# A bisection for the 256th largest index score: the wide tiles' search starts seven steps earlier, VectorE counts one of them, and the exact last step goes in pieces

## What is computed

```python
def dsa_attention(q, k, v, iq, ik, iw, table):
    ...
        logits = jnp.einsum('bqhd,bkd->bqhk', iqb, ik).astype(jnp.float32) * (IDX_DIM ** -0.5)
        score = jnp.einsum('bqhk,bqh->bqk', jax.nn.relu(logits), iwb)
        score = jnp.where(kpos[None, None, :] <= qpos[None, :, None], score, NEG)
        _, idx = lax.top_k(score, topk)
        valid = idx <= qpos[None, :, None]
    ...
        p = jax.nn.softmax(s, axis=-1)
```

## Time and profile before

| | us |
|---|---|
| median of 3 executions | 3599.42 (3598.71 to 3608.11) |
| the profiled execution's own time | 3598.85 |
| its span, first to last instruction | 3597.1 |
| TensorE busy | 3436.0 (96%) |
| VectorE busy | 1601.4 (45%) |
| ScalarE busy | 978.1 (27%) |
| mean granted TensorE clock | 0.983 of full |
| the loop of 64 steps, from the span's start | 1762.4 to 2398.6 |

### The profile page before, as it was taken

How to read it: one execution, slowest core, us unless ns; L and a number is a source line. 1 busy time by engine, 2 the same in 40 slices (tenths; PEclk the granted TensorE clock), 3 DMA queues, 4 the chain that set the end, 5 groups by cost and what they waited for, 6 DMA issues and landing times.

```text
span 3597.1 us, 31176 instructions
## 1 busy us (share of the span) xinstructions
PE 3436.0 (96%) x12370; PEld 1812.8 (50%) x12370; DVE 1601.4 (45%) x2938; ACT 978.1 (27%) x2059; POOL 93.6 (3%) x107
## 2 busy tenths in 40 slices
PE   7999999999999999999999999899999999999998
PEld 3556555555456444544566455564444444444443
DVE  2056191143156362552465563654336555253433
ACT  4244112002244111122577744531111000000001
POOL 0000000020000000100000000000110000000000
PEclk9999999999999999999999999899999999999999
DMA  5100121131000101111000101111000111101011
GB/s 209 54 6 13 58 88 62 53 108 38 27 7 13 34 27 53 41 44 41 36 24 30 39 21 56 62 45 44 29 24 35 47 47 35 47 35 47 35 41 65
DMA packets 49903, 163.72 MB, mean 46 GB/s; under 512 B 5296, under 2 KB 8624, under 8 KB 49085
## 3 DMA queue, kind: packets, MB, share of 16 engines
q1 hardware_dynamic: 44890, 145.82, 11.5%
q10 hardware_dynamic: 4868, 15.91, 1.3%
HBM read 157.46 MB, written 11.32 MB: 47 GB/s over the span
## 4 chain that ended last, share of the span: by engine, by line
PE 86%; DVE 7%; ACT 4%; issue 1%; SPq 1%; DMA 0%; POOL 0%; DVEq 0%; ACTq 0%; POOLq 0%
PE ps L551 34%; PE ps L1220 14%; PE ps L580 8%; PE ps L992 5%; PE ps L708 4%; PE ps L1003 2%; PE ps L731 2%; PE ps L887 2%; PE ps L720 2%; PE ps L1015 1%; PE ps L1070 1%; ACT sb L1756 1%; PE ps L1081 1%; DVE sb L2000 1%; PE ps L977 1%; PE ps L1098 1%
## 5 line engine op out<-in xcount | busy, mean ns | idle before, releaser
L551 PE MATMUL ps<-sb 128*128 128x512 f32 (+1 forms) x3088 | 1240.9, 563 | 14.0 <-ACT sb L1559 6.7
L551 PEld LDWEIGHTS ps<-sb 128*128 128x128 f32 x3088 | 589.3, 191 | 659.3 <-issue 633.8
L1279 ACT ACTIVATE sb<-ps 128x512 f32<-128x512 f32 (+10 forms) x709 | 350.6, 511 | 1522.9 <-PE ps L551 467.3
L1220 PE MATMUL ps<-sb 128*128 128x512 f32 x1232 | 531.3, 594 | 2.8 <-DVE sb L2626 2.8
L1220 PEld LDWEIGHTS ps<-sb 128*128 128x128 f32 x1232 | 234.6, 191 | 299.0 <-issue 293.5
L580 PE MATMUL ps<-sb 128*128 128x512 f32 x672 | 291.4, 594 | 2.4 <-ACT sb L1279 1.9
L992 PE MATMUL ps<-sb 128*128 128x512 f32 x512 | 231.3, 599 | 0.0
L580 PEld LDWEIGHTS ps<-sb 128*128 128x128 f32 x672 | 127.3, 190 | 163.2 <-issue 156.1
L1321 ACT ACTIVATE sb<-sb 128x512 f32<-128x512 f32 x128 | 74.7, 610 | 366.0 <-DVE sb L2573 122.5
L2136 DVE SCALAR_TENSOR_TENSOR sb<-sb 128x1310 f32<-128x1310 f32 (+1 forms) x120 | 161.7, 1424 | 0.0
L708 PE MATMUL ps<-sb 96*128 96x512 f32 (+1 forms) x400 | 155.3, 523 | 5.2 <-ACT sb L1468 4.5
(11 more groups left out here) (258 smaller groups left out, 3148.9 us busy)
## 6 DMA issues: line engine op xcount, KB each, us to landing
sb<-in_w_in SPq DMA_DIRECT2D x73, 512.0 KB, 3.3
sb<-in_w_ada SPq DMA_DIRECT2D x48, 512.0 KB, 4.6
sb<-in_w_up SPq DMA_DIRECT2D x44, 512.0 KB, 3.3
sb<-in_w_down SPq DMA_DIRECT2D x24, 384.0 KB, 3.1
sb<-in_w_out SPq DMA_DIRECT2D x16, 512.0 KB, 3.6
sb<-in_w_mkv SPq DMA_DIRECT2D x16, 512.0 KB, 3.3
rows_dram<-vec_dram ACTq DMA_DIRECT2D x1, 6906.0 KB
sb<-rows_dram ACTq DMA_DIRECT2D x6, 1024.0 KB, 5.1
```

The lines of the kernel that those rows point to most:

```text
L551: ins = mm(ps[:, 0:tn], w[:, k, :], src(k, t0, tn), start=(k == 0), stop=(k == nk - 1))
L1220: ins = mm(ps[:, 0:512], stationary(k), moving(k), start=(first and k == 0), stop=(k == 3), skip_group_check=not first)
L1279: return act(out, in_, func, scale=scale)
```

## The change

The group "high" begins at step 16, so that its passes fill steps 16 to 48. VectorE counts tile 7 (1024 columns) as it already counts tile 5, by the same instruction on the same scratch tile `marks`; ScalarE keeps tiles 2, 3, 4 and 6. `narrow` treats the last tile of either group in an instruction of its own. `keep_ranked` becomes a generator that stops after "at least", after the settling, and after each part but the last. `rank_pieces` advances it by two pieces ahead of `combine` or `normalise` and by one piece behind them, from step 34, 36, 38, 40, 50 and 53 on for tiles 2 to 7. Every write of the scratch tile waits for the last writer before it (`marked`). What is computed stays the same.

```diff
-SEARCH_AT = {"low": 0, "high": 23}
+SEARCH_AT = {"low": 0, "high": 16}
 PASSES = 33
-COUNTED = 5
-RANKED_AT = {34: 2, 36: 3, 38: 4, 40: 5, 57: 6, 59: 7}
+COUNTED = {"low": 5, "high": 7}
+RANKED_AT = {34: 2, 36: 3, 38: 4, 40: 5, 50: 6, 53: 7}
...
             count_signs("low", n, (4,))
-            count_signs("high", n, (6, 7))
+            count_signs("high", n, (6,))
...
-            if COUNTED in tiles:
-                j = COUNTED - 2
-                v.tensor_tensor(met[:, 0:j], tally[:, 0:j], goal[:, 0:j], ALU.is_ge).then_inc(*e.step())
-                stt(out=met[:, j:j + 1], in0=tally[:, j:j + 1], scalar=sense[:, j:j + 1], in1=goal[:, j:j + 1], op0=ALU.mult,
-                    op1=ALU.is_ge).then_inc(*e.step(("met", group, i)))
-            else:
-                v.tensor_tensor(met[:, g], tally[:, g], goal[:, g], ALU.is_ge).then_inc(*e.step(("met", group, i)))
+            a, j = g.start, COUNTED[group] - 2
+            v.tensor_tensor(met[:, a:j], tally[:, a:j], goal[:, a:j], ALU.is_ge).then_inc(*e.step())
+            stt(out=met[:, j:j + 1], in0=tally[:, j:j + 1], scalar=sense[:, j:j + 1], in1=goal[:, j:j + 1], op0=ALU.mult,
+                op1=ALU.is_ge).then_inc(*e.step(("met", group, i)))
...
-        def count_least(n):
+        marked = [None]
+
+        def mark(key):
+
+            marked[0] = key
+            return e.step(key)
+
+        def count_least(group, n):
...
+            e.wait_ge(*at(marked[0]))
+            v.tensor_scalar(marks[:, 0:w], sel(t), limit[group] if i else 0.0, 0.0, ALU.is_ge, ALU.add,
+                            accum_out=tally[:, j:j + 1]).then_inc(*mark(("counted", group, i, t)))
...
-        def keep_ranked(n):
-
-            if n not in RANKED_AT:
-                return
-            t = RANKED_AT[n]
+        ranking = [None]
+
+        def rank_pieces(n, pieces):
+
+            for _ in range(pieces):
+                if ranking[0] is None and n in RANKED_AT and ("sel", RANKED_AT[n]) not in steps.at:
+                    ranking[0] = keep_ranked(RANKED_AT[n])
+                if ranking[0] is not None and next(ranking[0], "kept") == "kept":
+                    ranking[0] = None
+
+        def keep_ranked(t):
+
...
+                if name == "at least":
+                    yield
...
             for p, (a, w) in enumerate(parts):
+                yield
...
             for piece in FILLERS.get((n, 0), ()):
                 filled(*piece)
+            rank_pieces(n, 2)
             if n < 32:
                 combine(n)
...
-            keep_ranked(n)
-            count_least(n)
+            rank_pieces(n, 1)
+            count_least("low", n)
+            count_least("high", n)
             if 1 <= n <= 32:
                 divide(n - 1)
```

More of the change, by code:

```diff
@@ L389, in program @@
     bound, found, power, tally, goal, met, sense, above, below, gap = [small[:, 128 + 6 * i:134 + 6 * i] for i in range(10)]
-    at_least, beyond, is_above, rank_value, rank_left, limit = [small[:, 188 + i:189 + i] for i in range(6)]
+    at_least, beyond, is_above, rank_value, rank_left = [small[:, 188 + i:189 + i] for i in range(5)]
+    limit = {"low": small[:, 193:194], "high": small[:, 194:195]}
     marks = view(KB0 + 2560, 256).bitcast(I8)
@@ L2259, in narrow @@
                     j, w = t - 2, (t + 1) * P
-                    v.tensor_scalar(met[:, j:j + 1], tally[:, j:j + 1], float(TOPK if t == COUNTED else 2 * TOPK - w), None,
+                    v.tensor_scalar(met[:, j:j + 1], tally[:, j:j + 1], float(TOPK if t == COUNTED[group] else 2 * TOPK - w), None,
                                     ALU.is_ge).then_inc(*e.step(("met", group, 0, t)))
@@ L2265, in narrow @@
                     v.tensor_scalar(sense[:, j:j + 1], met[:, j:j + 1], 2.0, -1.0, ALU.mult, ALU.add).then_inc(*e.step())
-                    span, low = (2 * TOPK - 1, 1 - TOPK) if t == COUNTED else (4 * TOPK - 2 * w - 2, w - 2 * TOPK + 2)
+                    span, low = (2 * TOPK - 1, 1 - TOPK) if t == COUNTED[group] else (4 * TOPK - 2 * w - 2, w - 2 * TOPK + 2)
                     v.tensor_scalar(goal[:, j:j + 1], met[:, j:j + 1], float(span), float(low), ALU.mult, ALU.add).then_inc(
@@ L2312, in narrow @@
             v.tensor_scalar(below[:, g], below[:, g], -1.0, None, ALU.mult).then_inc(*e.step(("turned ends", group)))
-        def count_least(n):
-            i, t = n - SEARCH_AT["low"], COUNTED
+        marked = [None]
[3 more added lines that the diff above has]
+        def count_least(group, n):
+            i, t = n - SEARCH_AT[group], COUNTED[group]
             if not 0 <= i < PASSES:
@@ L2322, in count_least @@
             else:
[L2323 to L2328, removed]
+                e.wait_ge(*at(("bound", group, i)))
+                stt(out=limit[group], in0=bound[:, j:j + 1], scalar=-1.0, in1=sense[:, j:j + 1], op0=ALU.mult,
+                    op1=ALU.mult).then_inc(*e.step(("limit", group, i)))
+                e.wait_ge(*at(("limit", group, i)))
+            e.wait_ge(*at(marked[0]))
+            v.tensor_scalar(marks[:, 0:w], sel(t), limit[group] if i else 0.0, 0.0, ALU.is_ge, ALU.add,
+                            accum_out=tally[:, j:j + 1]).then_inc(*mark(("counted", group, i, t)))
         def parts_of(t):
             return [(a, min(256, (t + 1) * P - a)) for a in range(0, (t + 1) * P, 256)]
-        def keep_ranked(n):
-            if n not in RANKED_AT:
-                return
-            t = RANKED_AT[n]
+        ranking = [None]
[6 more added lines that the diff above has]
+        def keep_ranked(t):
             j, x, parts = t - 2, sel(t), parts_of(t)
@@ L2347, in keep_ranked @@
                         e.wait_ge(*at(("at least", t, len(parts) - 1)))
+                    e.wait_ge(*at(marked[0]))
                     v.tensor_scalar(equal[:, 0:w], x[:, a:a + w], above[:, j:j + 1], total if p else 0.0, compare, ALU.add,
-                                    accum_out=total).then_inc(*e.step((name, t, p)))
+                                    accum_out=total).then_inc(*mark((name, t, p)))
+                if name == "at least":
+                    yield
             v.tensor_scalar(is_above, at_least, float(TOPK), None, ALU.is_ge).then_inc(*e.step(("is above", t)))
@@ L2367, in keep_ranked @@
                 stt(out=equal[:, 0:w], in0=count, scalar=rank_left, in1=equal[:, 0:w], op0=ALU.is_le, op1=ALU.mult).then_inc(
-                    *e.step(("first equal", t, p)))
+                    *mark(("first equal", t, p)))
                 e.wait_ge(*at(("first equal", t, p)))
```

## The result

The changed kernel takes 3580.66 us, median of 6 executions (3577.81 to 3583.53), against 3600.18 for the kernel before (6 executions). The ratio is 0.9942, with a 95% interval from 0.9932 to 0.9952: faster by 0.58%, where 3577.0 us, 0.6% less than before, had been forecast. The profiled execution took 3580.86 us.

The account below looks back on a forecast made before the run. TensorE, busy for 96% of the span, was taken as the bound, so only its idle time and clock in the loop could move. Terms -13.3 - 18 + 9.5 + 0 = -21.8 took 3598.85 us to 3577.0, range 3565 to 3592.

Parts of the forecast that it names:

- Term 1: Steps 38 to 41, rankings of tiles 4 and 5: splitting them removes the stalls of steps 39 and 41, -13.3 us.
- Term 2: Steps 56 to 63: rankings of tiles 6 and 7 leave steps 57 to 60, idle time and slow clock go, -18 us.
- Term 3: Steps 50 to 54: rankings of tiles 6 and 7 arrive where VectorE's work is the time, +9.5 us.
- Term 4: Steps 16 to 31: ScalarE's relief and VectorE's new count ahead of `divide` cancel, net 0.
- The two ends, -8 and +8: Steps 16 to 31: two thirds of TensorE's idle time gained, or VectorE's ring tighter than thought.
- Priced at nothing: Steps 32 to 47's exchange of counts, scratch-tile waits, DMA and a second `limit` column were taken to cost nothing.
- A: Rival: steps 16 to 31 clear up too and the memory sum runs at full clock, 3566 us; chance 0.15.
- B: Rival: backlog of steps 50 to 54 costs +16 to +20, or half the ranking stalls stay, 3584 to 3588; chance 0.2.
- C: Rival: slower, VectorE closes the ring of every step in steps 16 to 31, 3611 us; chance 0.07.

Follow-up runs that it names:

- pieces only: Kernel before with rankings split in pieces; wide tiles searched from step 23, counted by ScalarE, ranked from steps 57 and 59: 3577.53 us, ratio 0.9939.
- whole rankings: Changed kernel, but each ranking in one go at the end of its step (34, 36, 38, 40, 50, 53): 3605.01 us, ratio 1.0016.
- wide rankings late: Changed kernel, but rankings of tiles 6 and 7 run from steps 57 and 59 instead of 50 and 53: 3570.02 us, ratio 0.9921.
- thin and late: Changed kernel, but tiles 6 and 7 ranked from steps 55 and 58, one piece ahead of `normalise` instead of two: 3566.10 us, ratio 0.9908.
- thin from 50 and 53: Changed kernel, but for tiles 6 and 7 one ranking piece ahead of `normalise` instead of two, same starting steps: 3574.76 us, ratio 0.9927.
- the count in the wait: Changed kernel, but VectorE counts tile 7 right behind `narrow`, ahead of `combine` and `normalise`: 3574.52 us; two further versions add edits: 3562.53 and 3559.11 us.

## Why the prediction was right, point by point

The forecast's sum for the loop was -21.8 us. By the stretches the loop went from 623.5 to 601.8 us (step 0 to step 63), -21.7. That they agree to 0.1 is luck: terms 2 and 3 were off by 1.2 and 1.0 us in opposite directions. The profiled execution's own time fell by 18.0 and the median by 19.5, since the part before the loop, which the change does not touch, took 3.4 us more in the profiled execution. A stretch of it (1355 to 1470 us) shows why, first before, then after:

```profile
1355.00:1470.00 115.00, 107.86 (x397) 64.57 (x398) 33.92 (x60) 16.58 (x36) 14.55 (x18) 0.96 0.15 51
```

```profile
1355.00:1470.00 115.00, 108.89 (x392) 64.86 (x392) 30.36 (x55) 15.00 (x34) 12.67 (x16) 0.93 0.15 51
```

The granted clock is 0.03 lower over 115 us, which is 3.4 us of work: its falls there add up to 17.1 us instead of 10.2, and two of them lasted 6.8 us instead of 3.4. That is the difference between 3577 and the profiled 3580.86. There is one trace of each kernel, and the kernel before starts its loop earliest of all twelve (1762.4 us, the others 1764.5 to 1769.4), so whether its early start was luck is not shown.

- **Term 1, -13.3 forecast, -13.4 measured** (206.1 to 192.7). The steps came out at 13.4 and 14.1, as the even spacing of steps 37 to 43 had it. The run of pieces only and the run of whole rankings show it from both sides.
- **Term 2, -18 forecast, -16.8 measured** (87.4 to 70.6; steps 56 to 63: 100.0 to 83.2). The clock's part was 4 and came out at 4.5, TensorE's busy time from 85.97 to 81.50. The idle time was taken as gone whole, 14.0; 1.7 us of it stay, three short waits for ScalarE's copies in steps 56, 59 and 61.
- **Term 3, +9.5 forecast, +8.5 measured** (54.2 to 62.7). The distance between the two `normalise` was forecast as 50 us and is 49.03: 43.3 us of work where the sum had 45.0, the wait in step 52 at 3.3 where it had 4, and 2.4 us of small gaps where it had 1. The sign and the size were right, the reason was right only for this schedule: "here VectorE's work is the time" would give the same for whole and for thin rankings, and these took 74.4 and 54.7. VectorE's idle time in steps 50 to 55 is 18.4 us in the one, 7.5 in the full change and 2.3 in the other. What the sum did was follow the order of this one schedule, with the overlaps it has.
- **Term 4, 0 forecast, 0.0 measured** (144.6 and 144.6): -1.5 and +1.5 forecast, -1.7 in steps 24 to 31 and +1.7 in steps 16 to 23 measured. The first is by the mechanism that was named: 1.45 us for a count was 1.28 + 0.19, and `divide` starts behind it. The second has the right size at another wait: steps 20 to 23 got 0.3 to 0.6 us longer each, and TensorE waits there for ScalarE's eviction `back` (0.9 us, none before) and for `combine` (2.6 us, 1.9 before), not for `divide`. Each total holds one fall of the clock, before in step 31 and after in step 25, so they cancel. The two ends, -8 and +8, were not reached; the run in which ScalarE counts tile 7 shows +10 for the way not taken.
- **Priced at nothing**: ScalarE's and VectorE's exchange in steps 32 to 47 cost nothing. The waits for the last writer of the scratch tile appear nowhere in the rows.
- **The rivals**: A (steps 16 to 31 clear up) did not come, but its floor was real: another place for the same count takes 5.2 us off. B (the backlog is dearer) is what whole rankings would have met, and C did not come, since the odd steps' slack was used up by 0.3 to 0.6 us and not by more than one.
- **The price of the count**: 1277 ns for 1024 columns, against 1010 for 768, is 1.04 ns a column. The Trainium skill (VectorE: DVE Perf Modes, Mode 2×_2P) gives a `tensor_scalar` in fp32 from SBUF two elements a cycle; by the count's own row that does not hold for this form, which has an accumulator and writes int8, and the slope of the row decides. That points to the accumulator: with fp32 in and out, 256 columns take 514 ns with it (L2348 before) and 354 without, while the plain form's 753 ns for 1024 and 354 for 256 columns (L2455) are 0.52 ns a column, as the page has it.

## What to carry to other kernels

Split a long block of a queue before you move it: here splitting alone gave 25.0 us in the loop, and splitting and moving 21.7, since the move to short steps without independent TensorE work took 10 us back. Ask of every inserted instruction which wait of its own queue stands next to it; the same count cost 5 us less ahead of a wait than behind it, 1.7 of them by a fall of the clock that did not come. And write a stall down with the slow clock behind it, but don't read off the stall's length whether the fall comes.

## What the runs showed of the hardware

That a stall is followed by low clock was expected; that its length does not decide it was not. In nine traces the transposes of steps 25, 27, 29 and 31 come 1.7 to 2.9 us late, 36 stalls in all. Behind 11 of them the clock fell, for 3.4 us each time.

- In the five kernels that are the same up to step 33 (the change, wide rankings late, whole rankings, thin and late, thin from 50 and 53) it fell at step 25 (2.2 us) in all five, at step 27 (1.9 us) in one, at step 29 (1.8 us) in one, and at step 31 (1.7 us) in none. So at two of the four places the same instructions had it in one trace and not in another.
- In the three in which ScalarE counts tile 7 (before, pieces only, ScalarE counts tile 7) it fell at step 31 (2.3 us) in all three and never behind the longer stalls of steps 25 and 27 (2.4 to 2.9 us).
- Of the 12 stalls of 0.8 to 1.3 us at these places in the three runs with the count in the wait, none had a fall behind it.

A fall of 3.4 us moved the length of one step by 1.7 us. Before the loop the clock was at the lower level for 44 to 61 us in all, and the loop started between 1762 and 1769 us, in kernels that are the same up to there. What decides whether a fall comes, no run here shows.
